# Per-head norms by a block-ones product, an earlier modulation schedule and weight rings that outlive their stage in a two-layer hybrid mixer

## What is computed

```python
def _l2norm_heads(t):          # 8 heads of 64 channels
    th = _heads(t).astype(jnp.float32)
    th = th / jnp.maximum(jnp.sqrt(jnp.sum(jnp.square(th), axis=-1, keepdims=True)), 1e-12)
    return th.reshape(t.shape).astype(t.dtype)
...
a = sigmoid(a0 + ad @ a2)      # likewise the decay, from tanh(wd) @ w2
kk = _l2norm_heads(k * k_k)
```

## Time and profile before

| | |
|---|---|
| median of 3 runs | 3574.0 us (3571.06 to 3576.3) |
| the profiled execution | 3570.22 us, of which the span of the trace is 3568.4 us |
| mean granted TensorE clock | 0.973 of full speed |
| PE, busy share of the span | 93% |
| DVE, ACT, POOL | 44%, 37%, 33% |

### The profile page before, as it was taken

The page is one execution under the profiler, slowest core; times in us unless marked ns, Lnnn a source line. Parts: engine busy times, 40 slices in busy tenths (PEclk is TensorE's granted clock), DMA queues, the critical chain, the costliest instruction groups (busy, mean ns, idle before and its releaser), DMA issues. The chain is left out here.

```text
span 3568.4 us, 83214 instructions
## 1 busy us (share of the span) xinstructions
PE 3324.1 (93%) x36977; PEld 2718.2 (76%) x36977; DVE 1577.2 (44%) x2360; ACT 1321.9 (37%) x2364; POOL 1194.0 (33%) x757
## 2 busy tenths in 40 slices
PE   6999999999898999899999899999999898889998
PEld 4668888888776777787878776887777786668887
DVE  4234344443288556412112633445444396461324
ACT  3332243333276423421222343333443375343322
POOL 2111132232254412332333232123433274245553
PEclk8999999999999999999999999999999999999999
DMA  7663323442222342233332055333433323423332
GB/s 258 222 213 106 113 84 115 122 132 82 91 78 88 113 155 86 89 118 118 118 118 95 30 163 175 105 115 120 135 112 101 106 81 124 165 83 108 98 95 89
DMA packets 444863, 420.83 MB, mean 118 GB/s; under 512 B 15652, under 2 KB 372042, under 8 KB 437594
## 3 DMA queue, kind: packets, MB, share of 16 engines
q1 hardware_dynamic: 442922, 406.73, 35.8%
q10 hardware_dynamic: 1584, 8.78, 0.6%
HBM read 326.72 MB, written 88.74 MB: 116 GB/s over the span
## 5 line engine op out<-in xcount | busy, mean ns | idle before, releaser
L899 PE MATMUL ps<-I-336_h_hi,I-339_w_hi 128*128 128x256 f32 (+1 forms) x832 | 296.1, 356 | 4.5 <-PEq L124 4.5
L899 PE MATMUL ps<-I-337_h_lo,I-339_w_hi 128*128 128x256 f32 (+1 forms) x832 | 283.1, 340 | 0.0
L899 PE MATMUL ps<-I-336_h_hi,I-340_w_lo 128*128 128x256 f32 (+1 forms) x832 | 282.4, 339 | 0.0
L2492 POOL TENSOR_TENSOR I-19088_w_lo<-I-19086_w_raw,I-19087_w_hi 128x1024 fp32r<-128x1024 f32 x60 | 145.1, 2418 | 342.8 <-ACT I-19087_w_hi L2445 342.7
L899 PE MATMUL ps<-I-23849_h_hi,I-23852_w_hi 128*128 128x512 f32 (+1 forms) x544 | 211.7, 389 | 4.6 <-PEq L124 4.6
L899 PE MATMUL ps<-I-23850_h_lo,I-23852_w_hi 128*128 128x512 f32 (+1 forms) x544 | 199.8, 367 | 0.0
L899 PE MATMUL ps<-I-23849_h_hi,I-23853_w_lo 128*128 128x512 f32 (+1 forms) x544 | 199.7, 367 | 0.0
L2492 POOL TENSOR_TENSOR I-39610_w_lo<-I-39608_w_raw,I-39609_w_hi 128x1024 fp32r<-128x1024 f32 x60 | 144.4, 2407 | 154.6 <-ACT I-39609_w_hi L2445 154.6
L2445 ACT ACTIVATE I-19087_w_hi<-I-19086_w_raw 128x1024 fp32r<-128x1024 f32 x61 | 64.6, 1060 | 354.8 <-PE ps L381 235.0
L863 POOL TENSOR_TENSOR I-340_w_lo<-I-338_w_raw,I-339_w_hi 128x1024 fp32r<-128x1024 f32 x34 | 82.2, 2417 | 321.6 <-ACT I-339_w_hi L1143 321.6
L381 PE MATMUL ps<-I-19083_h_hi,I-19087_w_hi 128*128 128x512 f32 x704 | 183.2, 341 | 1.1 <-DVE I-19084_h_lo L413 1.1
(11 more groups left out here) (959 smaller groups left out, 9130.5 us busy)
## 6 DMA issues: line engine op xcount, KB each, us to landing
I-338_w_raw<-in_w_in SPq DMA_DIRECT2D x67, 512.0 KB, 5.6
I-23851_w_raw<-in_w_in SPq DMA_DIRECT2D x67, 512.0 KB, 5.2
I-19096_ada_w<-in_ada_w SPq DMA_DIRECT2D x24, 1024.0 KB, 6.0
I-19086_w_raw<-in_ffn_up SPq DMA_DIRECT2D x44, 512.0 KB, 3.9
I-39608_w_raw<-in_ffn_up SPq DMA_DIRECT2D x44, 512.0 KB, 3.8
proj_d<-I-2005_result SPq DMA_DIRECT2D x52, 384.0 KB, 2.9
I-513_ada_w<-in_ada_w SPq DMA_DIRECT2D x16, 1024.0 KB, 5.6
I-19086_w_raw<-in_ffn_down SPq DMA_DIRECT2D x22, 512.0 KB, 3.4
```

The costliest lines, as they stand in the source:

```text
L899: m = pe.matmul(bank(6 + i % 2, n_c), w[:, k, :], hv[:, k, c0:c0 + n_c], start=k == 0 and v == 0, stop=k == KT - 1 and v == 2)
L2492: pool.tensor_tensor(pair(g)[1], rings[0][:, g % 3, :, :], pair(g)[0].bitcast(F32), ALU.subtract).then_inc(sem("w_lo"), 1)
```

## The change

Seven edits, all shown below in their core.

1. The sums of kk squared are four products with `blkones` (ones in two 64 x 64 blocks), which give the sum of a head on all its 64 rows at once. ACT takes the root of each full 128 x 768 tile into kk; DVE takes the maximum, the reciprocal and the final multiplication of tile t after the shift of product 9 + t. The four spreading products, two small loads and the tiles `hd`, `hdT`, `inv` go.
2. The modulation steps run as `ada_at` says: one at each of the products 0 to 3, two at 4 and 5, one at 6 to 13. The copies move to products 5 and 13, the first flip to 7, the first addition to 9. SP's loads move with the steps; ring and waits stay as they are.
3. The gate's sigmoid moves from n = 8 to n = 9 on ACT.
4. One set of weight rings is allocated for the whole program.
5. The three first tiles of `ffn` are loaded at the end of `close`, those of layer 1's `rwkv_inputs` at the end of layer 0's `ffn`, under a semaphore `ahead`.
6. The statistics of the last tile are taken on DVE (`last_stats`).
7. `attention` ends with a root of one element on ACT.

```diff
@@ rwkv_inputs
+ada_at = [range(n + max(0, min(n - 4, 2)), n + max(0, min(n - 3, 2)) + 1) if ada and n < N - 1 else () for n in range(N)]
...
 for n in range(N):
-    load_weights(sp, sem, rings, n, ...)
+    if n >= 3 or not ahead:
+        load_weights(sp, sem, rings, n, ...)
...
-    if ada:
-        ada_load(sp, sem, ring, n, ada[n])
+    for e in ada_at[n]:
+        ada_load(sp, sem, ring, e, ada[e])
...
-    m = pe.matmul(side[0:HC, at:at + n], hd[:, t, :], kk[:, t, at:at + n], start=t == 0, stop=t == CTILES - 1)
+    m = pe.matmul(side[:, at:at + n], blkones[:, :], kk[:, t, at:at + n], start=True, stop=True)
-if p in SPREAD:
-    ...
-    m = pe.matmul(side[:, at:at + n], hdT[:, t, :], inv[:, at:at + n], start=True, stop=True)
...
-if ada:
-    ada_step(pe, sem, ring, n, 6)
-    if n == 9:
-        ada_flip(pe, sem, 0, 7)
+for e in ada_at[n]:
+    ada_step(pe, sem, ring, e, 6)
+if ada and n == 7:
+    ada_flip(pe, sem, 0, 7)
...
-if SUMS.get(p) == CTILES - 1:
-    act.wait_ge(sem("kk_ss"), 1)
-    act.activation(inv[:, :], side[0:HC, :], ACT.Sqrt).then_inc(sem("norm"), 1)
+if p in SUMS:
+    t = SUMS[p]
+    act.wait_ge(sem("kk_ss"), t + 1)
+    act.activation(kk[:, t, :], side, ACT.Sqrt).then_inc(sem("norm"), 1)
...
-if n == 8:
+if n == 9:
     act.wait_ge(sem("shifted"), 7)
     act.activation(gd[:, 0:width(R_G)], gd[:, 0:width(R_G)], ACT.Sigmoid).then_inc(sem("g_act"), 1)
 beside(2*n+1)
-if ada and n == 8:
-    ada_copy(act, sem, 0, 6)
+if ada and n in (5, 13):
+    ada_copy(act, sem, n // 13, 6)
...
 def normed(t):
+    k = kk[:, t, :]
+    dve.wait_ge(sem("norm"), t + 1)
+    dve.tensor_scalar(k, k, 1e-12, None, ALU.max).then_inc(sem("floor"), 1)
+    dve.wait_ge(sem("floor"), t + 1)
+    dve.reciprocal(k, k).then_inc(sem("inv"), 1)
+    dve.wait_ge(sem("inv"), t + 1)
+    dve.scalar_tensor_tensor(k, kf[:, t, :], col("kk", t), k, ALU.mult, ALU.mult).then_inc(sem("kk_done"), 1)
@@ attention, end of ACT's list
 o_copy(N - 1)
+act.activation(ratio[0:1, 0:1], ones[0:1, 0:1], ACT.Sqrt)
@@ close, end of SP's list (ffn of layer 0 likewise, for the next layer's w_in)
+for n in range(N - 3, N):
+    g = (n + KT) % 3
+    o = up_column(g // 2, g % 2)
+    sp.wait_ge(sem("w_lo"), n - 1)
+    sp.dma_start(raw(n), up[:, :, o:o + P]).then_inc(ahead, 16)
@@ close and ffn, end of ACT's and DVE's lists
 for t in range(nt):
     root(t)
-    next_stats(t)
+    if t < nt - 1:
+        next_stats(t)
...
+last_stats(dve, sem, st, mv, nt - 1)
@@ new
+def last_stats(dve, sem, st, mv, t):
+    dve.wait_ge(sem("xb"), t + 1)
+    for c in range(2):
+        m = dve.bn_stats(st[:, t, c, :], x[:, t, c * 512:(c + 1) * 512])
+    m.then_inc(sem("x_st"), 1)
+    dve.wait_ge(sem("x_st"), 1)
+    dve.bn_aggr(mv[:, t, :], st[:, t, :, :]).then_inc(sem("x_mv"), 1)
+    dve.wait_ge(sem("x_mv"), 1)
+    dve.tensor_scalar(x_nm[:, t:t + 1], mv[:, t, 0:1], -1.0, None, ALU.mult)
+    dve.tensor_scalar(x_ss[:, t:t + 1], mv[:, t, 1:2], float(D_MODEL), None, ALU.mult)
```

More of the change, by code:

```diff
@@ L465, in rwkv_inputs @@
             SUMS = {p: t for t, p in enumerate(range(14, 18))}
-            SPREAD = {p: t for t, p in enumerate((27, 28, 29, 30))}
-            with ExitStack() as s2, stage(nc) as (block, sem):
+            NORMED = {9 + t: t for t in range(CTILES)}
+            with ExitStack() as s2, stage(nc, [ahead] if ahead else ()) as (block, sem):
                 kfk = sb(s2, "k_and_kk", [P, 2, CTILES, TOK])
@@ L1916, in _, with close @@
                     split(KT + 1)
-        def close(l, oc, y, rings, last):
+        up_column = lambda j, i: (D_FF, 0)[i] + j * P
+        def close(l, oc, y, rings, last, ahead):
             seqs = LAT if last else BOTH
@@ L2261, in _, with ffn @@
                         scaled(t)
-        def ffn(l, h, last):
+                    last_stats(dve, sem, st, mv, nt - 1)
+        def ffn(l, h, rings, last, ahead, next_ahead):
             seqs = LAT if last else BOTH
@@ L2311, in ffn @@
             copy_at = {8 + 2 * (KT * u + KT - 1) + 1: u for u in range(len(ada) // KT)}
-            with ExitStack() as s2, stage(nc) as (block, sem):
-                rings = weight_rings(s2, 3, 2)
+            with ExitStack() as s2, stage(nc, (ahead,)) as (block, sem):
                 cv = sb(s2, "conv", [P, 2, TOK])
@@ L2362, in _ @@
                             ada_load(sp, sem, ada_ring, e, ada[e])
+                    if not last:
+                        src = A["w_in"][l + 1].rearrange("(k p) n -> p k n", p=P)
+                        for g in range(N, N + 3):
+                            o = OFF_C + MAINS[g % 3] * P
+                            slot_free(g)
+                            sp.dma_start(rings[0][:, g % 3, :, :], src[:, :, o:o + P]).then_inc(next_ahead, 16)
                     if last:
@@ L2484, in _ @@
                         root(t)
-                        if not last:
+                        if not last and t < nt - 1:
                             next_stats(t)
@@ L2578, in _ @@
                             scaled(t)
+                    if not last:
+                        last_stats(dve, sem, st, mv, nt - 1)
+        rings = weight_rings(top, 3, 2)
+        ahead = None
         for l in range(DEPTH):
@@ L2585, in program @@
                     h = activation_pair(s2)
-                    rings = weight_rings(s2, 3, 2)
-                    n_w = rwkv_inputs(l, h, rings, last)
+                    n_w = rwkv_inputs(l, h, rings, last, ahead)
                     with ExitStack() as s3:
@@ L2599, in program @@
                     merge_pa(l, oq, sm, ss, oc, y, rings, last)
[L2600 removed]
+                ahead = nc.alloc_semaphore(f"ffn_tiles_ahead{l}")
+                close(l, oc, y, rings, last, ahead)
             with ExitStack() as sc:
[L2602 removed]
+                used, ahead = ahead, None if last else nc.alloc_semaphore(f"input_tiles_ahead{l}")
+                ffn(l, activation_pair(sc), rings, last, used, ahead)
 _INS = ["x", "c", "ctx", "c_ctx", "ada_w", "ada_b", "w_in", "lam_qk", "subln_g", "tshift_mu", "rw_w0", "rw_w2", "rw_a0",
```

94 lines of the change are left out of this document (37 added, 57 removed).

## The result

| | before | after |
|---|---|---|
| median of 5 runs each | 3574.0 us (3571.06 to 3580.91) | 3555.15 us (3554.21 to 3555.95) |
| the profiled execution, its span | 3570.22, 3568.4 us | 3554.21, 3552.4 us |

The ratio is 0.9946, with a 95% interval of 0.9934 to 0.9958: 18.9 us faster in the median, 16.0 in the profiled executions.

What follows compares the result with a forecast made beforehand. PE, busy for 93% of the span, was taken as the bound. Terms of -7.7 + 15.4 + 1.9 - 6.0 - 4.7 + 2.3 - 2.4 - 1.3 - 1.2 = -3.7 us gave a median of 3570.3, range 3558 to 3582.

Steps and rivals of the forecast that it cites:

- new wait at product 5: Layer 0's input stage: PE waits 12.5 us for ACT, held by the late LoRA store, plus 2.9 half clock: +15.4.
- steps and gate's sigmoid, all: Input stages: old wait gone -7.7, new wait +15.4, two more steps before the last product's end +1.9, gate's sigmoid +2.3.
- spreading and stage end, layer 0: Layer 0's input stage: two spreading products fewer before the last main product's end, -3.0; kk stores leaving in a row, -3.5.
- the same, layer 1: Layer 1's input stage: two spreading products fewer, -3.0; kk stores leaving in a row at the end, -1.2.
- gate's sigmoid, tile 11, layer 1: Layer 1's input stage: weight tile 11, behind the gate's store on SP, makes product 11 late: +2.3, between nothing and 5.2.
- joints: statistics, tiles ahead, root: Stage joints: last tile's statistics on DVE -2.4, tiles loaded ahead -1.3, root's table loaded in ACT's idle time -0.6 a layer.
- The half clock after the new wait: Layer 0's input stage, after the wait at product 5: PE loses the same 2.9 us as at the old wait.
- the old wait's half clock: Layer 0's input stage: after step 8's 4.8 us wait for ACT's copy, 2.9 us lost; both gone, -7.7.
- The heads' sums: Input stages: new sums cost PE nothing, at most 1.5; two spreading products of 1.5 each go, -3.0 in each layer.
- The rival of 3554.9 us: Layer 0's input stage: transfers share engines instead of queueing, so the new wait's 15.4 us is absent; chance 0.25, half-wait case included.

Runs made afterwards that it cites:

- edits 2 and 3 alone: Kernel before with only the new order of modulation steps and the gate's sigmoid one product later; median 3583.91 us, ratio 1.0026.
- edit 1 alone: Kernel before with only the sums by `blkones` and no spreading products; median 3550.7 us, ratio 0.9936.
- edits 4 to 7 alone: Kernel before with only rings allocated once, tiles loaded ahead, last tile's statistics on DVE and the root ending attention; median 3571.45 us, ratio 0.9991.
- after with 8 products put back: Changed kernel plus eight 64-column products in each layer, ahead of the tiles' sums, which overwrite their results; median 3572.09 us, ratio 0.999.
- the version with the slices later: Changed kernel with SP's loads of modulation slices 7 and 8 moved behind weight tile 6 and the first LoRA store; median 3541.52 us, ratio 0.9913.
- the second profile of before: Kernel before, unchanged, profiled once more; 3577.5 us in one run.

## Why the prediction was wrong, point by point

| term of the sum | forecast | shown by | measured |
|---|---|---|---|
| new wait at product 5 | 12.5 idle | row at 131.61 | 13.48 |
| steps and gate's sigmoid, all | +11.9 | edits 2 and 3 alone | +8.6, interval 5 to 13 |
| spreading and stage end, layer 0 | -6.5 | edit 1 alone, against 198.4 to 201.6 | -3.1 to -6.3 |
| the same, layer 1 | -4.2 | edit 1 alone, against 162.5 to 163.0 | -5.2 to -5.7 |
| gate's sigmoid, tile 11, layer 1 | +2.3 | two waits before product 11 | 1.74 + 0.58 |
| joints: statistics, tiles ahead, root | -4.9 | edits 4 to 7 alone | -4.05, interval 0 to -6 |
| **sum** | **-3.7** | after with 8 products put back | **-3.4** |

*The terms came out near their measures.* Measured row by row they sum to -3.8 to -7.5, in the one kernel with eight products put back to -3.4 within 0 and -7. (One time of the forecast is off by 0.15 us, which changes nothing: its own terms for tile 11 give 2162.65, where it writes 2162.8.) ACT and SP hold up PE as the forecast had it, with tile 6 landing 16.1 us and the LoRA store 10.8 us after their issue; step 8 has no wait; the scan's first product follows the last v product 3.25 us sooner (235.98 to 246.78 for 229.26 to 243.31, 3 to 4 forecast). The wait of 1.74 on ACT before product 11 is there with edits 2 and 3 alone (1.75) and not with edit 1 alone. Rows don't matter to the reciprocal, as assumed: 4.95 us on 128 rows, 4.94 on 8, and no product from 10 on waits for DVE. The root's table comes early:

```profile
1134.00 1.28 ACT L1591 ACT_TABLE_LOAD   x1
1135.30 0.20 ACT L1591 ACTIVATE I-13905_ratio<-I-51_ones 1x1 f32<-1x1 f32 x1
1136.89 0.24 ACT L1815 ACTIVATE I-16582_head_rstd<-I-16582_head_rstd 128x48 f32<-128x48 f32 x1 [1.39 <-DVE I-16582_head_rstd L1866]
...
2137.76 4.95 DVE L669 RECIPROCAL I-23865_k_and_kk<-I-23865_k_and_kk 128x768 f32<-128x768 f32 x1
```

*The new wait is as long as forecast in part by luck.* The forecast moved the whole sequence of the kernel before on SP, 22.0 us from the issue of slice 5 to the landed LoRA store, to a later start. But in that sequence SP was held by PE for 7.9 us, until a modulation step ended at 94.6, and not by transfers. Here are the kernel before and, below it, the changed one:

```profile
93.53 1.04 PE L180 MATMUL ps<-I-513_ada_w,I-65_silu_c 128*2 128x512 f32 x8
94.63 0.33 SPq L171 DMA_DIRECT2D I-513_ada_w<-in_ada_w  x1
```

```profile
106.31 1.90 PE L178 MATMUL ps<-I-510_ada_w,I-65_silu_c 128*2 128x512 f32 x16
```

In the changed kernel the step that slice 8 needs was over at 108.2, before SP came to it at 109.66, and still its issuing took 9.24 us. No wait of the list held SP there; `x_keep` and tile 6 were still under way. In the version with the slices later, a k store in the same place, second behind `x_keep`, took 8.02 us to issue (98.51 to 106.53). Nothing ties the two holds to each other; that they last about as long is luck.

*Two sizes were off.* The half clock after the new wait was 0.59 for 4.4 us (131.6 to 136.0), 1.8 us lost instead of 2.9. And the old wait's half clock, 2.9 in the sum, is not always there: the second profile of before has a stage 3.2 us shorter.

*The step that failed* is the costing of "The heads' sums": "PE moves the same columns for the sums, so I cost the new ones at nothing", and the spreading products at "1.5 each". I priced instructions by their duration only. Taking eight products out of PE's list in each layer moved every later product against the cuts of the list, and that was worth 16 to 17 us, as much as the largest term of the sum and more than four times the sum itself. The trace of before had it in the first row of PE's list of waits, 25.5 us of "issue" at one line in 19 waits, and I left it unread because the diff doesn't touch the scan. The rival of 3554.9 us has the right time by luck: its mechanism, no new wait, is refuted by the row at 131.61.

*Left open:* what makes a block's packet start sooner or later after PE has passed the cut before (0.4 to 3.4 us at the stalls over 0.6 us of the first scans, 2.3 us or more at all ten that are longer than 2.4), why a product waits another 1.1 to 1.6 us once the packet has landed, and why the median moved by more than the first scan.

## What to carry to other kernels

Before costing an edit of PE's list, read the waits whose releaser is "issue": if bursts of small products stall at places a fixed number of products apart, any product added or removed ahead of them shifts these places, and a gain or loss from that says nothing about the edit itself. Put the removed instructions back as work of no use (or take the same number away) to tell the two apart, and look for idle time in which some more of them are free. And compare stages that the diff leaves alone over two profiles of the same kernel: here the joints differed by 5.4 us, some 3 of them at one place where the low clock lasted longer.

## What the hardware showed that was not expected

- PE's list stalls PE at fixed places, 127 products (254 with their weight loads) apart, when the cut falls near the end of a burst of 192 products of 64 columns. Each stall of over 0.6 us ends 1.1 to 1.6 us after a 16 KB packet of the instruction queue has landed. From 3 products behind the burst's end on, the first scan shows 1.1 us at most and mostly under 0.6; right at the end it shows up to 1.5. A cut in the first 94 products of a burst showed no stall of 0.6 us in the first scan; in the second scan one 91 products in did (1.94 us).
- The place is fixed, the length varies: the stall at product 1356 took 0.71 us in one profile of the kernel before and 1.45 in the other. How far a kernel's runs scatter does not follow from the places: the changed kernel's five lie within 1.7 us, the five with the slices later, whose places are the same, within 13.9, and the 21 of the kernel before within 13.3.
- Issuing one transfer took 9.24 us (slice 8) and 8.02 us (a k store of 384 KB) where it was the second behind the 3 MB of `x_keep`; the other single issues in the rows shown here took 0.3 to 1.3.
- Small products alone in an idle stretch are slow: 109 ns each for 64 columns at a granted clock of 0.50 and 88 ns for 32 columns at 0.64, all with the same weights and the same output; inside a burst, at a granted clock of 1.00 and with weights and outputs that change, 32 of them with 64 columns end 0.65 us after the first begins. The clock explains a factor of two at most; the rest was not followed.
